# Four-strip recurrence levels, far levels read by ScalarE, and a weight split between two halves of a gate

## The reference, cut to what matters

```python
f = lb + (1.0 - lb) * jax.nn.sigmoid(z)            # hg_logf, per direction; then max(f, F_MIN)
a = jnp.cumsum(gi, axis=2)                         # hgrn2_scan, gi = log f
att = jnp.einsum('bhnd,bhmd,bhnmd->bhnm', qi, ki, jnp.exp(a_n - a_m))   # for m <= n
o = jnp.einsum('bhnm,bhme->bhne', att, vi) + jnp.einsum('bhnd,bhde->bhne', qi * jnp.exp(a), s)
p = jax.nn.softmax(s, axis=-1); o = jnp.einsum('bhqk,bkhd->bqhd', p, v)  # branch B
out = jnp.sum(sigmoid(mg) * proj, axis=2) @ w_o    # proj: each branch times w_br
```

## Time and profile before

| | us |
|---|---|
| median of 3 runs | 1671.99 (1671.47 to 1674.47) |
| the profiled execution | 1672.74 |
| its span | 1670.8 |
| TensorE busy | 1576.2 (94%) |
| VectorE busy | 1029.3 (62%) |
| ScalarE busy | 785.5 (47%) |
| GpSimd busy | 124.8 (7%) |

### The profile page before, as it was taken

How to read it: one execution, slowest core, us unless ns; L and a number is a source line. 1 busy time by engine, 2 the same in 40 slices (tenths; PEclk the granted TensorE clock), 3 DMA queues, 4 the chain that set the end, 5 groups by cost and what they waited for, 6 DMA issues and landing times.

```text
span 1670.8 us, 20677 instructions
## 1 busy us (share of the span) xinstructions
PE 1576.2 (94%) x8312; PEld 1211.2 (72%) x8312; DVE 1029.3 (62%) x1026; ACT 785.5 (47%) x893; POOL 124.8 (7%) x85
## 2 busy tenths in 40 slices
PE   4999999999999999999989899999999999999997
PEld 1778888777778767888877786676676666666676
DVE  2654798665444565479866875555555555555566
ACT  4534533454333553453335665545444444444465
POOL 1100133000000020023300000000000000000000
PEclk8999999999999999999999999999999999999999
DMA  9875544378774467554434699999999999999992
GB/s 396 316 300 191 193 152 152 113 277 297 287 273 152 151 248 300 191 193 152 151 114 194 243 334 397 389 380 385 396 358 372 401 404 389 376 395 396 381 399 78
DMA packets 56256, 470.63 MB, mean 282 GB/s; under 512 B 6400, under 2 KB 6448, under 8 KB 9056
## 3 DMA queue, kind: packets, MB, share of 16 engines
q1 hardware_dynamic: 53712, 461.27, 72.0%
q0 software_dynamic: 2448, 8.01, 1.3%
HBM read 465.05 MB, written 4.19 MB: 281 GB/s over the span
## 4 chain that ended last, share of the span: by engine, by line
PE 79%; DVE 8%; ACT 7%; DMA 3%; issue 2%; POOL 0%; ACTq 0%; POOLq 0%; DVEq 0%; SPq 0%
PE ps L1268 21%; PE ps L1270 20%; PE ps L1269 20%; DVE ring_lo L2363 6%; ACT w_hi L944 5%; PE ps L1752 3%; PE ps L1237 2%; PE ps L1371 2%; PE ps L1469 1%; DMA ring<-in_w_in 1%; PE ps L1344 1%; PE ps L1734 1%; PE ps L1713 1%; PE ps L1286 1%; DMA ring<-in_w_mod 0%
## 5 line engine op out<-in xcount | busy, mean ns | idle before, releaser
L2363 DVE TENSOR_TENSOR ring_lo<-ring,w_hi 128x2048 fp32r<-128x2048 f32 x197 | 448.0, 2289 | 143.9 <-ACT w_hi L944 143.8
L1268 PE MATMUL ps<-ring_lo,h_both 128*128 128x512 f32 x1032 | 410.3, 398 | 9.8 <-issue 6.4
L944 ACT ACTIVATE w_hi<-ring 128x2048 fp32r<-128x2048 f32 x197 | 373.0, 1911 | 67.5 <-PE ps L1270 63.2
L924 ACT ACTIVATE ring_lo<-ring 128x2048 fp32r<-128x2048 f32 x90 | 172.2, 1915 | 197.8 <-PE ps L1270 187.9
L2277 DVE TENSOR_TENSOR ring_lo<-ring,ring_lo 128x2048 fp32r<-128x2048 f32 x74 | 177.8, 2408 | 118.7 <-ACT ring_lo L924 118.0
L1268 PEld LDWEIGHTS ps<-ring_lo,h_both 128*128 128x128 f32 x1032 | 193.8, 188 | 60.0 <-issue 16.6
L1270 PE MATMUL ps<-ring_lo,h_both 128*128 128x512 f32 x592 | 230.8, 390 | 0.0
L1269 PE MATMUL ps<-ring_lo,h_both 128*128 128x512 f32 x592 | 230.5, 389 | 0.0
L1270 PE MATMUL ps<-w_hi,h_both 128*128 128x512 f32 x440 | 171.7, 390 | 0.0
L1269 PE MATMUL ps<-w_hi,h_both 128*128 128x512 f32 x440 | 171.4, 390 | 0.0
L1268 PE MATMUL ps<-ring_lo,act_hi 128*128 128x512 f32 x308 | 126.2, 410 | 26.8 <-DVE ring_lo L2363 23.2
(11 more groups left out here) (385 smaller groups left out, 2039.8 us busy)
## 6 DMA issues: line engine op xcount, KB each, us to landing
ring<-in_w_ff SPq DMA_DIRECT2D x297, 1024.0 KB, 7.2
ring<-in_w_in SPq DMA_DIRECT2D x36, 2048.0 KB, 9.0
u<-in_w_mod SPq DMA_DIRECT2D x21, 2048.0 KB, 9.0
ring<-in_w_br SPq DMA_DIRECT2D x6, 2048.0 KB, 7.7
ring<-in_w_o SPq DMA_DIRECT2D x4, 2048.0 KB, 7.6
ring<-in_w_mod SPq DMA_DIRECT2D x3, 2048.0 KB, 16.7
out<-state_out POOLq DMA_DIRECT2D x4, 512.0 KB, 5.6
x_sb<-in_x SPq DMA_DIRECT2D x1, 1024.0 KB, 10.6
```

The source lines that it names most:

```text
L924: A(hi, ring[s][:, half * UNIT:(half + 1) * UNIT], ACT.Copy).then_inc(mix_hi, 1)
L944: A(part_hi(p, n), ring[slab_slot(n)][:, p * UNIT:(p + 1) * UNIT], ACT.Copy).then_inc(hi_ready[p], 1)
L1268: mm(out, a_hi, b_lo, start=start, stop=False, skip_group_check=True)
L2363: V.tensor_tensor(ring_lo[slot][:, part], ring[slot][:, part], part_hi(p, n).bitcast(F32), ALU.subtract)\
```

## The change

1. `level` works in four strips of 32 positions. For every u and strip s it multiplies 32 columns of `k_lev` with 32 columns of `q` (64 at level 6) and writes PSUM partitions 32 s to 32 s + 31: 32 products of 128x32 stationary columns in place of 8 of 128x128. Levels 0 to 4 and 7 take the strip's own columns, level 5 the neighbour strip's, level 6 the other half's. Levels 0 to 6 write bank 6 only.
2. Levels 0 to 4 are read by VectorE into a new tile `hnear` of 8 x 32 columns, under masks of a quarter of the width. Levels 5 and 6 are read by ScalarE with plain copies (`levels_far`), after it has copied `hnear` onto the diagonal blocks of `hatt`. Level 7 is read as before.
3. `attention_out` goes to ScalarE, after its work for panel 11; the inverse of the sums stays on VectorE. The scale-and-add of `forget` goes to ScalarE, behind the sigmoid.
4. `gated` is called for each half: the low half stands ahead of `ahead(l, "br", n)`, the high half behind it.
5. The level masks are loaded by five DMAs (`diagonal` and four strips of `near_mask`) in place of one.

```diff
-                    pool.dma_start(level_mask, levels).then_inc(s_level, 16)
+                    pool.dma_start(diagonal, levels[:, NLEV, :]).then_inc(s_level, 16)
+                    for s in range(P // STRIP):
+                        rows = slice(s * STRIP, (s + 1) * STRIP)
+                        pool.dma_start(near_mask[rows], levels[rows, 0:5, rows]).then_inc(s_level, 16)
...
+            def attention_out(l):
+
+                act.wait_ge(pt0_read, l + 1)
+                act.wait_ge(pv_done, l + 1)
+                for u in range(8):
+                    hc = slice((u % 4) * HD, (u % 4 + 1) * HD)
+                    ins = A(br[:, 1, u // 4, hc], ps[:, 4 + u // 4, hc], ACT.Copy, scale=pinv[:, u:u + 1])
+                ins.then_inc(br_ready, 1)
+
+            def levels_far(l, v):
+
+                if v == 5:
+                    act.wait_ge(lev_read, 8 * l + 5)
+                    for s in range(P // STRIP):
+                        rows = slice(s * STRIP, (s + 1) * STRIP)
+                        A(hatt[rows, :, rows], hnear[rows], ACT.Copy)
+                act.wait_ge(lev_done, 8 * l + v + 1)
+                for s in range(P // STRIP if v == 5 else 2):
+                    width = STRIP if v == 5 else 2 * STRIP
+                    rows, cols = (slice(b * width, (b + 1) * width) for b in (s, s ^ 1))
+                    ins = A(hatt[rows, :, cols], ps[rows, 6, 0:8 * width].rearrange("p (u t) -> p u t", u=8), ACT.Copy)
+                ins.then_inc(lev_read, 1)
...
+                    if j == 16:
+                        levels_far(l, 6)
...
+                    if j == 15:
+                        levels_far(l, 5)
...
+                    if j == 11:
+                        attention_out(l)
...
-                        A(dst, ps[:, 6:8, :], ACT.Sigmoid).then_inc(t_read_act, 1)
+                        link(A(dst, ps[:, 6:8, :], ACT.Sigmoid))
+                        for h in range(H):
+                            part, c = dst[:, :, h * HD:(h + 1) * HD], 4 * (q - 5) + h
+                            ins = A(part, part, ACT.Identity, scale=olb[:, l, c:c + 1], bias=lb[:, l, c:c + 1])
+                        ins.then_inc(t_read_act, 1)
...
+                width = 2 * STRIP if v == 6 else STRIP
                 for u in range(8):
-                    ins = mm(ps[:, 6 + u // 4, (u % 4) * P:(u % 4 + 1) * P], k_lev[:, u * P:(u + 1) * P],
-                             q[:, u * P:(u + 1) * P], start=True, stop=True)
+                    for s in range(P // STRIP):
+                        rows = slice(s * STRIP, (s + 1) * STRIP)
+                        first = {5: (s ^ 1) * STRIP, 6: (1 - s // 2) * 2 * STRIP}.get(v, s * STRIP)
+                        if v == NLEV:
+                            out = ps[rows, 6 + u // 4, (u % 4) * P + first:(u % 4) * P + first + width]
+                        else:
+                            out = ps[rows, 6, u * width:(u + 1) * width]
+                        ins = mm(out, k_lev[:, u * P + s * STRIP:u * P + (s + 1) * STRIP],
+                                 q[:, u * P + first:u * P + first + width], start=True, stop=True, skip_group_check=True)
...
-            def attention_out(l):
+            def sums_inverse(l):
                 dve.wait_ge(p1_ready, l + 1)
                 dve.wait_ge(p0_ready, l + 1)
-                link(V.reciprocal(pinv, psums))
-                dve.wait_ge(pv_done, l + 1)
-                for u in range(8):
-                    hc = slice((u % 4) * HD, (u % 4 + 1) * HD)
-                    ins = V.tensor_scalar(br[:, 1, u // 4, hc], ps[:, 4 + u // 4, hc], pinv[:, u:u + 1], None, ALU.mult)
-                ins.then_inc(br_ready, 1)
+                V.reciprocal(pinv, psums)
...
                 dve.wait_ge(t_read_act, 2 * l + d + 1)
-                for h in range(H):
-                    v = f.rearrange("p (g h t) -> p g h t", g=2, h=H)[:, :, h, :]
-                    c = 4 * d + h
-                    ins = V.tensor_scalar(v, v, olb[:, l, c:c + 1], lb[:, l, c:c + 1], ALU.mult, ALU.add)
-                link(ins)
...
-                dve.wait_ge(s_level, 16)
-                V.copy_predicated(hatt.rearrange("p (u t) -> p u t", u=8),
-                                  level_mask[:, v, :].unsqueeze(1).broadcast_to([P, 8, P]),
-                                  ps[:, 6:8, :].rearrange("p b (h t) -> p (b h) t", h=H)).then_inc(lev_read, 1)
+                dve.wait_ge(s_level, 16 * 5)
+                if v == NLEV:
+                    V.copy_predicated(hatt, diagonal.unsqueeze(1).broadcast_to([P, 8, P]),
+                                      ps[:, 6:8, :].rearrange("p b (h t) -> p (b h) t", h=H)).then_inc(lev_read, 1)
+                else:
+                    V.copy_predicated(hnear, near_mask[:, v, :].unsqueeze(1).broadcast_to([P, 8, STRIP]),
+                                      ps[:, 6, 0:8 * STRIP].rearrange("p (u t) -> p u t", u=8)).then_inc(lev_read, 1)
...
-            def gated(l, n):
+            def gated(l, n, half):
 
                 if n:
                     dve.wait_ge(brt_done, 4 * l + 2)
                 dve.wait_ge(win_read, NWIN * l + 14 + 2 * n)
-                for half in range(2):
-                    dve.wait_ge(pr_done, 6 * l + 2 * n + half + 1)
-                    cols = slice(half * 512, (half + 1) * 512)
-                    src = ps[:, 2 * half:2 * half + 2, :]
-                    dst = merged[:, :, cols] if n == 0 else br[:, 1]
-                    ins = V.tensor_tensor(dst, src, gates[:, :, cols], ALU.mult)
-                    own(ins, pr_read, 6 * l + 2 * n + half + 1)
-                    if n:
-                        link(V.tensor_tensor(merged[:, :, cols], merged[:, :, cols], br[:, 1], ALU.add))
+                dve.wait_ge(pr_done, 6 * l + 2 * n + half + 1)
+                cols = slice(half * 512, (half + 1) * 512)
+                src = ps[:, 2 * half:2 * half + 2, :]
+                dst = merged[:, :, cols] if n == 0 else br[:, 1]
+                ins = V.tensor_tensor(dst, src, gates[:, :, cols], ALU.mult)
+                own(ins, pr_read, 6 * l + 2 * n + half + 1)
+                if n:
+                    link(V.tensor_tensor(merged[:, :, cols], merged[:, :, cols], br[:, 1], ALU.add))
...
                 ahead(l, "win", 10)
+                sums_inverse(l)
                 dve.wait_ge(pt0_done, l + 1)
                 V.tensor_copy(pT0.rearrange("p h t -> p (h t)"), ps[:, 4, :]).then_inc(pt0_read, 1)
                 forget(l, 1, f_suf, k_b)
                 products(l, 0)
                 ahead(l, "win", 11)
-                attention_out(l)
                 level_read(l, 0)
...
                 level_read(l, 2)
                 products(l, 3)
+                gated(l, 0, 0)
                 ahead(l, "br", 0)
-                gated(l, 0)
+                gated(l, 0, 1)
                 level_read(l, 3)
                 products(l, 4)
                 ahead(l, "win", 14)
@@ -2724,11 +2764,10 @@
                 level_read(l, 4)
                 products(l, 5)
                 ahead(l, "win", 15)
-                level_read(l, 5)
                 products(l, 6)
+                gated(l, 1, 0)
                 ahead(l, "br", 1)
-                gated(l, 1)
-                level_read(l, 6)
+                gated(l, 1, 1)
                 products(l, NLEV)
                 ahead(l, "win", 16)
                 level_read(l, NLEV)
```

More of the change, by code:

```diff
@@ L48 @@
 NLEV = 7
+STRIP = 32
 HEAVY, RANKED, LIGHT = 5, E - 2, P // 2
@@ L224, in program @@
         b_prex, q_lev, k_lev = (u2[:, i * D:(i + 1) * D] for i in range(3))
-        hatt = u2[:, 4 * D:5 * D]
+        hatt = u2[:, 4 * D:5 * D].rearrange("p (u t) -> p u t", u=8)
+        hnear = u2[:, 3 * D:3 * D + 8 * STRIP].rearrange("p (u t) -> p u t", u=8)
         act_s = u[:, 0:2 * W].rearrange("p (t c) -> p t c", t=2)[:, :, 0:FS]
@@ L240, in program @@
         pickT_light = pickT_light.rearrange("p (c g m) -> p c g m", c=2, g=2)
-        (state0, cache, level_mask, hgn_sb), (pick_light, x_light, corner, _) = shared(
-            [("state0", 2 * W), ("cache", 2 * W), ("level_mask", 8 * P), ("hgn_sb", W)],
+        (state0, cache, near_mask, diagonal, hgn_sb, _), (pick_light, x_light, corner, _) = shared(
+            [("state0", 2 * W), ("cache", 2 * W), ("near_mask", 5 * STRIP), ("diagonal", P), ("hgn_sb", W), ("mixer_rest", 736)],
             [("pick_light", 2 * 7 * LIGHT), ("x_light", KD * 3 * LIGHT), ("corner", W), ("light_rest", 640)])
@@ L249, in program @@
         cv = cache[:, W:2 * W]
-        level_mask = level_mask.bitcast(I32).rearrange("p (v t) -> p v t", v=8)
+        near_mask = near_mask.bitcast(I32).rearrange("p (v t) -> p v t", v=5)
+        diagonal = diagonal.bitcast(I32)
         con = sb("con", NCONST)
@@ L1964, in recurrence_out @@
                         u = 4 * g + h
-                        ins = mm(ps[:, 6 + g, hc], hatt[:, u * P:(u + 1) * P], rv_hi[:, g, hc], start=True, stop=(g == 0))
```

(1 more changed line is left out.)

## The result

The changed kernel takes 1650.66 us in the median (1649.40 to 1652.22), against 1671.73 for the kernel before in the same comparison: a ratio of 0.9871, with an interval of 0.9860 to 0.9883, or 21 us. The profiled execution has a span of 1648.7 us, 22.1 less than before.

The account below looks back on a forecast made before the run. TensorE, with 79% of the chain, was taken as the bound. Per layer 3.6 + 7.5 - 4.1 = 7.0 us, both layers 14.0, gave 1658.0 us against the median of 1671.99; the 8 in 10 range was 1651 to 1667.

Parts of the forecast that it names:

- part 4: Token mixer, panels 9 to 17: waits, mainly from the port shared by VectorE and GpSimd, give back 4.1 us a layer.
- the project's wait: `project` waits for ScalarE's read of the panel before, which the shorter level no longer covers: twice 0.3 us a layer.
- part 1: Gate's low half read ahead of VectorE's split ends TensorE's breaks at panels 14 and 16: 3.6 us a layer.
- part 2: Level matmuls in four strips side by side: 0.80 us a level for 1.79, `level` 6 1.22; gain 7.5 us a layer.
- B: Rival: small level matmuls run one after another, 27 ns each, a level 2.03 us; 1668.6 us in all; chance 0.20.
- C: Rival: the sequencer paces level matmuls at 58 ns, a level takes 4.0 us; 28 us slower, 1700; chance 0.09.
- Panel 14: At its start TensorE, there at 241.8, waits for VectorE's low-half read, ended at 242.5: 0.8 us charged.
- Panel 16: GpSimd takes the port before VectorE's split; TensorE waits 0.1 us at the start and 2.6 at the second half.
- rival A2: At panel 16 VectorE's split gets the port ahead of GpSimd's; 2.6 us a layer not given back, 1652.8; chance 0.16.
- my list: Four engines' operations from `level` 0 written side by side with the rows' durations, to find who waits for whom.
- The shift is kept to the end: After `level` 7 everything hangs on TensorE's progress, so the 14.0 us won in both layers last to the end.
- part 3: ScalarE takes 11.5 us a layer of new work, covered by its waits for TensorE; VectorE is relieved; counted as nothing.

Follow-up runs that it names:

- one_strip: Changed kernel with all level products written to PSUM partitions 0 to 31, so all 64 matmuls of a level share one strip of the array: 1673.23 us.
- early_project: Changed kernel; project's first 12 matmuls no longer wait for ScalarE's read of the last panel, only the second 12 do: 1660.22 us.
- gate_only: Kernel before with only the gate order changed: each half called for itself, the low half ahead of the split: 1667.43 us.
- late_split: Changed kernel with one more VectorE operation of 1.2 us between the sum of branch 1's low half and the split behind it: 1662.86 us.
- dve_far: Changed kernel with the near and far copies of `levels_far` moved from ScalarE to VectorE: 1661.54 us.
- dve_scales: Changed kernel with `attention_out` and the scale-and-add of `forget` back on VectorE: 1657.50 us.
- early_add_late: `early_project` with VectorE's sum of branch 1's low half moved behind its split: 1651.85 us.
- levels_only: Changed kernel with the split ahead of both halves of the gate again: 1663.31 us.

## Why the forecast was off, step by step

The step that failed is part 4, what the change gives back. I charged 4.1 us a layer; the trace has 1.4. The term that was mis-sized is the project's wait, 0.3 us for 0.7. With the 0.09 us by which each level was too short it made TensorE and ScalarE late enough that VectorE was in time at panels 14 and 16, where I had charged 0.8 and 2.7 us. Outside my sum altogether were 3.7 us that the profile shows beyond the changed stretch.

- **The gates (part 1).** 3.6 us a layer forecast; the two breaks were 1.88 and 1.85 us, 3.7 together, and are gone. Right.
- **The levels (part 2).** Forecast 0.80 us a level against 1.79; measured 0.69 from first to panel, 0.09 more for entering the shape and 0.11 for the panel's second matmul, so 0.89, and 1.24 at `level` 6 against 1.22. 6.8 us a layer, not 7.5: 0.09 us too little a level, 0.05 because I had the group at 30 ns where it takes 33, and 0.04 because what is paid once a level is 0.36 and not 0.32. Rivals B and C are out; it is the reading of rows 6 and 7 as "the array paces, the sequencer does not" that held, and `one_strip` shows what B would have been. The Trainium skill's rule (TensorEngine Tiling (Array Packing), Instruction Overhead: some 60 cycles a matmul) does not agree with four strips here: 8 ns a matmul are under the 25 ns that I had worked out from it. In one strip, at 33 ns, they are not.
- **The project's wait (part 4).** Forecast 0.3 us twice; measured 0.7 twice (`level` 2 and 5 take 1.40 in place of 0.69). I had counted ScalarE's two reads at 1.1 us, and 1.08 they are; but from the last panel matmul to the next stage it is 1.72 (panel 13: TensorE's last matmul starts at 228.25, ScalarE's reads at 228.67, and TensorE goes on at 229.97), so 0.42 before the reads and 0.22 behind them come on top. This is the term that was mis-sized.
- **Panel 14 (part 4).** 0.8 us forecast (by the list's own times, 242.5 and 241.8, it is 0.7), 0.1 measured. The same step: VectorE's read ended at 241.76, and TensorE, later by the project's wait and three levels, was through with `level` 3 at 241.75 (241.06 and 0.69). In `early_project`, without that wait, TensorE waits 0.71 us here.
- **Panel 16 (part 4).** 2.7 us a layer forecast, nothing measured; rival A2, at 0.16, is what happened. The mechanism was right (`gate_only`, `late_split`, `early_project` and `dve_far` all show it, at 2 to 3 us), its direction in this kernel was not. I had VectorE ready at 280.6 and ScalarE's split ended at 280.0; they came at 279.76 and 280.2, in a stretch that began 0.64 us sooner. Counted from the start of `level` 0 (204.74 in the trace that my list was made from, 204.10 now), VectorE came at 75.7 us where I had 75.9, and ScalarE at 76.1 where I had 75.3. ScalarE was 0.8 us later than in my list: 0.8 more for the two waits of project, 0.5 more for six levels, and some 0.7 less at panel 14 make 0.6 of it. A list that is good to 0.3 us cannot decide a race with a margin of 0.6, and I gave the two sides 0.48 and 0.16. `early_project` shows that the project's wait decides the order: with it taken away VectorE still starts its split at 75.7, but GpSimd starts at 75.5 in place of 76.2 and is first, as in my list.
- **The sum.** 3.6 + 6.8 - 1.4 = 9.0 a layer by these terms, 9.2 by the rows; forecast 7.0.
- **The shift is kept to the end.** Forecast as exact. It is not: 3.7 us more came from outside in the profile, the greater part from the clock at 361 and 856 us, 1.6 us each. Why the clock stays up there is open. This was no term of my sum at all, and with A2 alone (1652.8) I would still have been 2 us high.
- **ScalarE takes its share for nothing (part 3).** Right: it still waits for TensorE ahead of its splits (37.1 us for 22 of them from 170 to 320 us, in place of the 55.1 of the earlier trace rows), and what it took off VectorE turned out to be needed, 5 to 7 us (`dve_scales`) and 9 to 11 us (`dve_far`), which I had counted at nothing for TensorE.

## What to carry to other kernels

When two engines exclude one another on a port and a split of 4.6 us is in the game, whoever is first by a tenth decides over 2 to 3 us of the bound engine, and a list made from durations cannot tell who; price both outcomes equally, or make the order sure by putting the operation that is waited for ahead of those that are not (`early_add_late` against `early_project`: one sum moved, 3.6 us in the stretches). Before a gain of 1 or 2 us is worked on, look at the granted clock behind the waits of the whole kernel: some 1.4 to 1.6 us come and go at each such place, between kernels that differ only far from it and between executions of one kernel. Parts of a change that relieve the same engine should be measured together and apart: here 5 and 9 us apart were 19 to 21 together.

## What was not expected of the hardware

- Groups of four 128x32 by 32 matmuls in four strips start every 33 ns, that is 8 ns a matmul; in one strip each takes 31 to 33 ns by itself (64 in 2.14 us, with or without the 0.16 that is paid once). The modulation's 58 ns a matmul said nothing about the sequencer.
- A wait of TensorE of 2.75 us was followed by half clock, 1.3 to 1.6 us lost (`late_split`); one of 1.76 us in `gate_only` was not; one of 2.1 us was in `dve_far` and was not in `early_project`; one of 2.18 us in `levels_only` was in layer 1 (780 us) and was not in layer 0 (244 us); and at the same place behind the same wait of 1.88 us it was either, by the kernel: half before the change, full in both executions after it.
